# Rotary embedding of two attention layers: partner rows fetched by SBUF-to-SBUF DMAs in place of a TensorE permutation

## The reference, cut to what matters

```python
# layer a: halves of a 64-wide head, also for the index queries qi and the index key ki
def apply_rope(x):
    x1, x2 = x[..., :half], x[..., half:]
    return concatenate([x1 * c - x2 * sn, x1 * sn + x2 * c])

# layer c: neighbours of a head, after an RMS norm of every head
def apply_rope_2(x, cos, sin):
    x1, x2 = xp[..., 0], xp[..., 1]
    return stack([x1 * c - x2 * s, x1 * s + x2 * c])
```

## Time and profile before

| | before |
|---|---|
| median of 3 runs | 2630.72 us (2630.54 to 2632.61) |
| the profiled execution's own time | 2627.3 us |
| its span, first to last instruction | 2626.0 us |
| mean granted TensorE clock | 0.992 |
| PE busy | 2568.1 us (98%) |
| DVE, ACT, POOL busy | 1290.3, 979.4, 1244.5 us |
| DMA | 274.48 MB, mean 105 GB/s |

### The profile page before, as it was taken

How to read it: one execution, slowest core, us unless ns; L and a number is a source line. 1 busy time by engine, 2 the same in 40 slices (tenths; PEclk the granted TensorE clock), 3 DMA queues, 4 the chain that set the end, 5 groups by cost and what they waited for, 6 DMA issues and landing times.

```text
span 2626.0 us, 33091 instructions
## 1 busy us (share of the span) xinstructions
PE 2568.1 (98%) x13418; PEld 2077.3 (79%) x13418; DVE 1290.3 (49%) x2151; ACT 979.4 (37%) x1620; POOL 1244.5 (47%) x618
## 2 busy tenths in 40 slices
PE   8989999999999999999999999999999999999999
PEld 6667888888777888888777888888888888888887
DVE  4873899842135499982566431222336233431221
ACT  4474423223347432233367432232324223432231
POOL 4874544444456444444467344443433443444442
PEclk9999999999999999999999999999999999999999
DMA  4202555532220355542210233322422222233322
GB/s 147 65 18 80 169 192 189 187 106 66 97 80 10 124 189 185 188 157 96 87 35 18 81 96 96 96 97 91 142 96 80 97 88 88 82 96 97 98 98 78
DMA packets 259435, 274.48 MB, mean 105 GB/s; under 512 B 6868, under 2 KB 249300, under 8 KB 259028
## 3 DMA queue, kind: packets, MB, share of 16 engines
q1 hardware_dynamic: 259284, 272.37, 32.1%
HBM read 270.26 MB, written 2.10 MB: 104 GB/s over the span
## 4 chain that ended last, share of the span: by engine, by line
PE 87%; DVE 7%; ACT 2%; issue 2%; POOL 1%; DMA 0%; SPq 0%; DVEq 0%
PE bank L457 22%; PE bank L458 22%; PE bank L459 22%; DVE acc L1394 2%; PE bank L640 2%; PE bank L525 2%; PE bank L527 2%; PE bank L526 2%; PE bank L595 2%; PE bank L433 2%; DVE tmp L1429 2%; PE bank L434 2%; PE bank L437 1%; PE bank L623 1%; DVE Hlo L1432 1%
## 5 line engine op out<-in xcount | busy, mean ns | idle before, releaser
L1738 POOL TENSOR_TENSOR wlo<-raw,whi 128x1024 fp32r<-128x1024 f32 (+1 forms) x408 | 989.4, 2446 | 1192.7 <-ACT whi L926 1192.6
L457 PE MATMUL bank<-Xhi,whi 128*128 128x512 f32 (+1 forms) x1616 | 640.8, 397 | 1.5 <-POOL wlo L1738 1.5
L458 PE MATMUL bank<-Xlo,whi 128*128 128x512 f32 (+1 forms) x1616 | 630.0, 390 | 0.0
L459 PE MATMUL bank<-Xhi,wlo 128*128 128x512 f32 (+1 forms) x1616 | 629.2, 389 | 0.0
L926 ACT ACTIVATE whi<-raw 128x1024 fp32r<-128x1024 f32 (+1 forms) x408 | 404.9, 1041 | 570.0 <-PE bank L459 495.6
L457 PE MATMUL bank<-Hhi,whi 128*128 128x512 f32 x1024 | 400.6, 391 | 0.0
L458 PE MATMUL bank<-Hlo,whi 128*128 128x512 f32 x1024 | 399.0, 390 | 0.0
L459 PE MATMUL bank<-Hhi,wlo 128*128 128x512 f32 x1024 | 398.4, 389 | 0.0
L457 PEld LDWEIGHTS bank<-Xhi,whi 128*128 128x128 f32 (+1 forms) x1616 | 302.2, 187 | 73.5 <-issue 8.1
L459 PEld LDWEIGHTS bank<-Xhi,wlo 128*128 128x128 f32 (+1 forms) x1616 | 302.4, 187 | 65.4
L458 PEld LDWEIGHTS bank<-Xlo,whi 128*128 128x128 f32 (+1 forms) x1616 | 302.4, 187 | 64.9 <-issue 3.2
(11 more groups left out here) (273 smaller groups left out, 3119.0 us busy)
## 6 DMA issues: line engine op xcount, KB each, us to landing
ada<-in_ada_w SPq DMA_DIRECT2D x48, 1024.0 KB, 5.2
raw<-in_w_up SPq DMA_DIRECT2D x32, 1024.0 KB, 5.7
raw<-in_w_down SPq DMA_DIRECT2D x32, 1024.0 KB, 5.1
raw<-in_mlp_w_in SPq DMA_DIRECT2D x32, 1024.0 KB, 5.6
raw<-in_mlp_w_out SPq DMA_DIRECT2D x32, 1024.0 KB, 5.1
raw<-in_gmlp_w_in SPq DMA_DIRECT2D x24, 1024.0 KB, 5.0
raw<-in_gmlp_w_out SPq DMA_DIRECT2D x12, 1024.0 KB, 5.1
raw<-in_w_in_a SPq DMA_DIRECT2D x8, 1024.0 KB, 5.2
```

The costliest lines, as they stand in the source:

```text
L457: pe.matmul(b[0:rows, :], whi[s][:, c, j:j + rows], hi[:, c, :], start=(c == 0), stop=False)
L458: pe.matmul(b[0:rows, :], whi[s][:, c, j:j + rows], lo[:, c, :], start=False, stop=False)
L459: m = pe.matmul(b[0:rows, :], wlo[s][:, c, j:j + rows], hi[:, c, :], start=False, stop=(c == KC - 1))
L1738: pool.tensor_tensor(wlo[u % 2][:, c0:c1, 0:k], src[:, c0:c1, 0:k], whi[u % 2][:, c0:c1, 0:k].bitcast(F32), ALU.subtract).then_inc(lo_done, 1)
```

## The change

Both permutation matrices, their loads and the 25 PE rotations go. A new function `swap(r)` on ACT, called right after the tile has been copied to `held`, waits for that copy, waits until DVE has read the tile of rotation r-3, and issues DMAs from SBUF to SBUF that copy row blocks of the held tile to their partners' partitions: four DMAs of 32 partitions for layer a (two for r = 2), two of every second partition for layer c. They land in one of three new tiles (`SWA`, `SWC`), each with its own semaphore. DVE's sine product reads that tile in place of PSUM bank 4; POOL's cosine product, which works in place, waits for the landing as it waited for PE. For the keys of layer c the swap stands in ACT's order ahead of the evacuation of query tiles 2 and 3.

```diff
+    swap_in = [sem(f"swap_in{i}") for i in range(3)]
...
+    def swap_pieces(r):
+
+        if r >= 15:
+            return [(slice(h, P, 2), slice(1 - h, P, 2)) for h in range(2)]
+        return [(slice(o, o + 32), slice(o ^ 32, (o ^ 32) + 32)) for o in range(0, 64 if r == 2 else P, 32)]
+
+    def swapped(r):
+
+        landed = sum(len(swap_pieces(x)) for x in range(r % 3, r + 1, 3))
+        return (SWA if r < 15 else SWC)[r % 3], swap_in[r % 3], 16 * landed
...
-        def rotation(r, p, rows=P):
-            if r < 15:
-                pe_until.wait_ge(held_in, r + 1)
-            elif ROT_C[r][0] == "q":
-                pe_until.wait_ge(held_in, 18 + ROT_C[r][1])
-            else:
-                pe_until.wait_ge(hn_out, ROT_C[r][1] + 1)
-            if r == 0:
-                pe_until.wait_ge(const_in, 64)
-            else:
-                pe_until.wait_ge(rot_sin, r)
-            pe.matmul(bank[4][0:rows, :], perm[p][0:rows, 0:rows], rotated(r)[0:rows, :], start=True, stop=True).then_inc(rot_full, 1)
-
...
         def after_ki(o):
-            rotation(1, 0)
             pe_until.wait_ge(vec_in, 16 * (len(vec_rows) - 1))
-            pe_until.wait_ge(rot_sin, 2)
...
+        def swap(r):
+
+            tile, landing, _ = swapped(r)
+            if r >= 3:
+                act_until.wait_ge(rot_sin, r - 2)
+            for dst, src in swap_pieces(r):
+                act.dma_start(tile[dst, :], rotated(r)[src, :]).then_inc(landing, 16)
+
         def hold(name, r0, rows=P):
...
                 act.activation(held[r % 3][0:rows, :], bank[g % 4][0:rows, :], ACT_F.Copy).then_inc(held_in, 1)
+                act_until.wait_ge(held_in, r + 1)
+                swap(r)
             return evacuate
...
+            if o in (2, 3):
+                act_until.wait_ge(hn_out, o - 1)
+                swap(ROT_C_AT["k", o - 2])
             wait_tile(g)
...
             act.activation(tmp[o % 2][:], bank[g % 4][:], ACT_F.Square).then_inc(held_in, 1)
+            act_until.wait_ge(held_in, 18 + o)
+            swap(ROT_C_AT["q", o])
         units("qc", evac_qc)
...
         def rotation_sin(r, rope, rows=P):
-            dve_until.wait_ge(rot_full, r + 1)
+            tile, landing, whole = swapped(r)
+            dve_until.wait_ge(landing, whole)
...
-            dve.tensor_tensor(tmp[2 + r % 2][0:rows, :], bank[4][0:rows, :], rope[0:rows, 1, :], ALU.mult).then_inc(rot_sin, 1)
+            dve.tensor_tensor(tmp[2 + r % 2][0:rows, :], tile[0:rows, :], rope[0:rows, 1, :], ALU.mult).then_inc(rot_sin, 1)
...
         def rotation(r, rope, rows=P):
-            pool_until.wait_ge(rot_full, r + 1)
+            _, landing, whole = swapped(r)
+            pool_until.wait_ge(landing, whole)
```

More of the change, by code:

```diff
@@ L143, in body @@
     rcol, zcol, FG, GS = sb("rcol", [P, 2 * NT]), sb("zcol", [P, 2 * NT]), sb("FG", [P, KC]), sb("GS", [P, KC])
-    perm = [sb(f"perm{i}", [P, P]) for i in range(2)]
     pick, warm = sb("pick", [P, 19]), sb("warm", [P, 1])
@@ L195, in body @@
         rope_a = sb("rope_a", [P, 2, S], F32, region)
+        SWA = [sb(f"SWA{i}", [P, S], F32, region) for i in range(3)]
     Hhi, Hlo, ada, gained = [], [], [], None
@@ L215, in body @@
         rope_b = sb("rope_b", [P, 2, S], F32, region)
+        SWC = [sb(f"SWC{i}", [P, S], F32, region) for i in range(3)]
         KH = [sb(f"KH{i}", [P, S], F32, region) for i in range(2)]
@@ L251, in body @@
         sem(n) for n in ("set_done", "xsq_done", "vec_full", "vec_set", "silu_exp", "silu_step"))
-    held_in, rot_full, rot_sin, rot_cos, rot_sum, rot_sump, key_copy, wi_full, wi_set = (
-        sem(n) for n in ("held_in", "rot_full", "rot_sin", "rot_cos", "rot_sum", "rot_sump", "key_copy", "wi_full", "wi_set"))
+    held_in, rot_sin, rot_cos, rot_sum, rot_sump, key_copy, wi_full, wi_set = (
+        sem(n) for n in ("held_in", "rot_sin", "rot_cos", "rot_sum", "rot_sump", "key_copy", "wi_full", "wi_set"))
+    swap_in = [sem(f"swap_in{i}") for i in range(3)]
     idx_full, idx_relu, idx_acc, idx_wt, idx_add, sel_step = (sem(n) for n in ("idx_full", "idx_relu", "idx_acc", "idx_wt", "idx_add", "sel_step"))
@@ L673, in tensor_program @@
         pe_until.wait_ge(vec_set, 1)
-        rotation(0, 0)
         def after_ki(o):
-            rotation(1, 0)
             pe_until.wait_ge(vec_in, 16 * (len(vec_rows) - 1))
-            pe_until.wait_ge(rot_sin, 2)
             pe.transpose(bank[4][:, 0:114], R1, ident[0:114, 0:114]).then_inc(vec_full, 1)
@@ L685, in after_qj @@
             if o:
-                rotation(3, 0)
                 return
@@ L692, in after_qj @@
             m.then_inc(wi_full, 1)
-            rotation(2, 0, 64)
         fm("qj", X, chunk_a, after_qj)
@@ L711, in after_qa @@
         def after_qa(o):
-            rotation(4 + o, 0)
             for i, heads in INDEX_AFTER.get(o, ()):
@@ L715, in tensor_program @@
         fm("qa", X, chunk_a, after_qa)
[L717 to L720, removed]
+        fm("ka", X, chunk_a)
+        tm("va", chunk_a)
         pe_until.wait_ge(idx_relu, 24)
@@ L817, in after_qc @@
             query_means(o - 1)
-            if o in (3, 4):
-                rotation(ROT_C_AT["k", o - 3], 1)
-            rotation(ROT_C_AT["q", o - 1], 1)
         fm("qc", X, lambda c: wait_chunk("c", c), after_qc)
@@ L830, in after_vc @@
                 query_means(7)
-                rotation(ROT_C_AT["q", 7], 1)
             if o == 2:
@@ L1566, in vector_program @@
         dve.tensor_tensor(PBB[7][:].rearrange("p (i c h) -> p i c h", c=8, h=16), *copies, ALU.subtract).then_inc(lf_dve, 1)
-        dve_until.wait_ge(const_in, 64)
+        dve_until.wait_ge(const_in, 32)
         dve.tensor_copy(PICK[:], pick[:, 0:16]).then_inc(ck_dve, 1)
@@ L1862, in sync_program @@
             sp.dma_start(dst, src).then_inc(vec_in, 16)
-        for dst, name in ((head_mean, "head_mean"), (perm[0], "perm_half"), (perm[1], "perm_pair"), (pick, "pick")):
+        for dst, name in ((head_mean, "head_mean"), (pick, "pick")):
             sp.dma_start(dst[:], consts[name]).then_inc(const_in, 16)
@@ L1913, in shape_constants @@
     rope_a = np.stack([np.tile(c, (4, 1)), np.concatenate([-s, s, -s, s])], 1)
[L1914 to L1917, removed]
     tok = np.arange(S)
@@ L1934, in shape_constants @@
         "ident": np.eye(P, dtype=f), "head_mean": np.kron(np.eye(2), np.full((64, 64), 1 / 64)).astype(f),
-        "perm_half": perm_half, "perm_pair": perm_pair, "pick": pick,
+        "pick": pick,
         "rope_a": rope_a.astype(f), "rope_b": rope_b.astype(f), "tri": tri, "tsum": tsum,
```

## The result

| | before | after |
|---|---|---|
| median | 2630.63 us (4 runs, 2629.64 to 2632.61) | 2641.86 us (4 runs, 2639.92 to 2642.22) |
| ratio, 95% interval | | 1.0042 [1.0029, 1.0054] |
| the profiled execution's own time, its span | 2627.3, 2626.0 us | 2641.91, 2640.6 us |
| mean granted TensorE clock | 0.992 | 0.981 |

What follows compares the result with a forecast made beforehand. It took PE to bound layer c and saturated DVE to set layer a's end. Layer a's 4.5 + 1.9 + 5.0 = +11.4 and layer c's -9.8 gave +1.6, so 2632.3 us, range 2620 to 2641 (forecast's own 2626 to 2636).

Steps and rivals of the forecast that it cites:

- The bound: Before the change, PE sets layer c's time; layer a's end is set by 57.3 us of saturated DVE.
- Layer c, -9.8: Layer c: rotations off PE save 10.8 us, 1.0 charged behind the last query tile, ACT's issues otherwise hidden: -9.8 us.
- Layer a, first step, +4.5: Layer a up to the first scores: ACT's issues and DVE's waits for POOL delay rotation 4's sum, +4.5 us.
- Layer a, second step, +1.9: Layer a, query tiles 1 and 2 with scores: ACT's issues delay the relus PE's fourth score waits for, +1.9 us.
- Third step, +5.0: Layer a's saturated DVE stretch: seven sine products wait about 0.8 us each for POOL, +5.0 us.
- The sum: Layer a +11.4 and layer c -9.8 give +1.6 us in the whole kernel, median 2632.3 us.
- (1) PE bounds everything: Whole kernel: all PE savings count, -25 us, some 2606; chance 0.04.
- (2) Layer a breaks even: Layer a: port waits mostly fall in idle moments and ACT's issues are cheap; total -8 to -6, 2623 to 2625; chance 0.23.
- (3) Late landing: POOL's first cosine and layer c's end: swaps land in 5.2 us, not 1.9; total +7.5, 2638; chance 0.23.
- (4) The four pieces land one after the other: A tile's four swap DMAs land serially, 7.6 us; +8.5 on top of +1.6, 2641; chance 0.05.
- The signs: Expected profile marks: no line 577, layer c tiles 6.36 us apart, sine product median near 1.3, memset near 94, attention near 157.

Runs made afterwards that it cites:

- c_only: Only layer c swapped by DMA as in the changed kernel, layer a's rotations left on PE as in the kernel before: 2619.0 us, ratio 0.996.
- filler: Changed kernel plus 60 matmuls with unused results where PE would wait for ACT's relus: 2630.3 us, -11.5 against the changed kernel.
- sp_issue: Changed kernel with layer a's swap DMAs issued by SP between its weight loads instead of ACT: 2626.5 us, -15.3 against the changed kernel.
- port_only: Kernel before, with DVE's sine product of layer a reading two SBUF tiles, no DMA added: 2634.6 us, ratio 1.0019, +4.5.
- psum_sine: Changed kernel with the sine table copied into PSUM bank 4, so the sine product has one PSUM operand: 2637.1 us, -4.8 against the changed kernel.
- sp_psum: Changed kernel with layer a's swaps issued by SP and the sine table copied into PSUM bank 4: 2619.8 us, 22.1 below the changed kernel.
- issue_only: Kernel before plus layer a's 58 DMAs issued by ACT into unread tiles, POOL waiting for their landing: 2640.6 us, ratio 1.004, +10.4.
- one_piece: Changed kernel with one DMA per rotation in layer a, rows copied but not swapped: 2629.05 us, -12.8 against the changed kernel.

## Why the prediction was wrong, point by point

**The bound.** Right in what it read: layer c is PE's, and layer a before the change was DVE's. It took for granted that layer a stays DVE's. After the change the rows from 90 to 140 us show DVE at 1.7 to 6.7 of 10 in three of them: between 77 and 131 us the chain goes through ACT's issues and PE, and only from 134 us on through DVE.

**Layer c, -9.8.** Measured -10.2 in after and in c_only between the same instructions, and -11.1 in c_only's median. Tiles 6.4 apart as worked out (6.36), with or without a key rotation. The issues on ACT cost 1.15 per tile and not 0.9, hidden all the same.

**Layer a, first step, +4.5.** Near in size: the sum of rotation 4 began at 66.07 where 65.6 was worked out, behind DVE's wait of 3.46 for POOL's cosine. Part of that is luck. The `qj` tiles did not end where they were but 4.2 and 3.2 us later (evacuated at 49.40 and 55.43, before 45.19 and 52.21), because PE paused for `wlo`, which the step has at 2.5 us and not 4.0, and then ran 13 matmuls at the low level, which it does not have:

```profile
41.06 0.76 PE L470 MATMUL bank<-Xhi,whi 128*128 128x512 f32 x1 [4.01 <-POOL wlo L1742]
```

So `wlo` began at 59.70 and not 57.9. Against that, cosine 5 did not run ahead of sum 4 but beside it, and held it up: the sum took 1.74 us in place of 0.69 and ended 6.3 us later than before.

**Layer a, second step, +1.9. This is the step that failed**, and with it the third. PE's pause was worked out and charged at its own length, and what comes behind the pause was put at nothing, without a reason. The runs showed TensorE at its low level there for 6 to 7 us: 3.1 us of each tile, by the trace of after and by filler. From rotation 4's sum to the memset it was 33.4 us where it was 26.7, +6.6 in place of +1.9.

The end of the pause came out right by two errors that cancel. The step took 0.37 us per issue, "the row that also moves 64 KB", and 0.43 as the upper bound, both from SP's loads out of DRAM; these SBUF-to-SBUF issues took 0.61 on ACT (0.59 on SP, in sp_issue), so the relu came 3.2 us behind the evacuation and not 2.2. But the step also let the fourth score wait for the second relu. In both kernels (`idx_relu, n - 2`) it waits for the first relu of its four, which comes 1.1 us earlier. So the fourth score could start 3.7 us behind the evacuation, 3.8 by the step; it ended at 5.4 and not at 4.3, because it took 1.65 us at the low level, where 0.5 was put down and 0.91 is what the high level gives.

**Third step, +5.0.** Its mechanism was right: 4.5 us in port_only, 4.8 in psum_sine, the longest product 2.67 us, their mean 1.33. But from the memset to the attention it was 69.3 us in place of 58.6, +10.7. "What PE saves in tiles 3 and later is lost in waiting for DVE" had the wrong sign there: three more tiles came 13.5 to 13.8 us apart (8.8 to 9.5 before), and DVE waited for them. Part of DVE's wait for POOL is hidden by that, so the prices measured one at a time (low clock 11.5 in filler, issues and clock together 15.3 in sp_issue, POOL 4.8 in psum_sine) are not parts of one sum; the last two together gave 22.1 in sp_psum.

**The sum.** +1.6 became +11.2 by medians, and 2641.86 lies just above the range's 2641. Layer a was put at +11.4 and was +22.6 in the trace; the difference, 11.2, is about what filler gives back (11.5) with nothing but a fuller PE. Whether it is that to the last microsecond can't be said: filler also changes when scores come.

**The rivals.** (1) PE bounds everything: false. (2) Layer a breaks even: false. Its "issues on ACT are cheap" is refuted by issue_only. (3) Late landing: false as a cause. Three rotations of 15 did land as late as a weight load, but the median is 2.1 us [1.9 in rows 9], and sp_psum, where landings take up to 4.8 us too, has no loss in layer a. Its sign came out, by another mechanism. (4) The four pieces land one after the other, 7.6 us: false as a delay of landing, since the median piece lands 2.1 us after its own issue and issues are 0.6 apart; that its 2641 is near the measured time is luck. The advice of the Trainium skill's page "DMA: Bandwidth & Descriptors", section "Rules for kernel authors", to use one transfer for two to disjoint partitions, agrees with one_piece in what it saves, 12.8 us, though there by the issues that it spares; one_piece only copies the rows.

**The signs.** No more line 577, ACT's issues between evacuation and relu, tiles of layer c, the maximum of the sine product: as said. Its median in layer a was 0.78 and not 1.3, but the mean of the 128-row products was 1.33: the 0.8 us was worked out as a mean, and some products meet no POOL instruction while others wait for most of one. The memset came at 99 and not 94, the attention at 169 and not 157. The text named an issue cost above 0.5 us as what would make it wrong, and it was above. The low clock was in no sign.

On DVE and POOL the Trainium skill's page "SBUF — State Buffer", section "SBUF: two separate sides", states an exclusive lock: a DVE operation with two SBUF inputs and a GpSimd operation that reads SBUF keep each other out for the whole instruction. By that rule the trace agrees: 0.68 us alone and up to 2.67 beside POOL's `wlo` with two SBUF inputs, never above 0.692 once one of the two lay in PSUM (psum_sine).

## What to carry to other kernels

A DMA issue is work of the engine that issues it, at its own measured price for its kind (0.6 us here, where the loads took 0.30 to 0.43): look at what stands behind it on that engine, and issue from a queue where nobody waits. Where an edit makes PE wait for about two microseconds in every tile, charge the matmuls after the wait at the low level as well (waits of 1.0 to 1.7 us mostly went without it here); filling the wait with matmuls for nothing shows, in one run, how much that is. And where DVE and POOL are both full, keep one operand of DVE's two in PSUM. Before charging a wait, look up in the kernel which increment it waits for.

The two best kernels are c_only, 2619.0 us, which leaves layer a alone, and sp_psum, 2619.8, both 0.4% under before.

## What the runs showed of the hardware that was not expected

TensorE's granted clock fell to its low level, 1.2 of 2.4 GHz, after pauses of PE of only 1.9 to 2.3 us, in four tiles of four (ends at 80.79, 94.24, 107.81 and 121.66), and stayed there for another 6 to 7 us of work, with matmuls 0.43 us apart in place of 0.23, though PE's busy share in the stretch from 80 us was 92%. In one_piece, where PE hardly pauses behind the evacuation, the same stretch had 1.00. In issue_only five pauses of 1.0 to 1.7 us were followed by the low level once, for 3.4 us. The shortest pause in after that was followed by it, and the one in issue_only:

```profile
107.81 1.92 PE L703 MATMUL bank<-KI,QI 64*128 64x512 f32 x2 [1.89 <-ACT TA L1070]
```

```profile
77.48 0.91 PE L720 MATMUL bank<-KI,QI 64*128 64x384 f32 x2 [1.40 <-ACT TA L1088]
```

The issue of an SBUF-to-SBUF DMA of 32 partitions x 2 KB holds the issuing engine for 0.51 us as the first of a group and 0.61 as each next one on ACT, and for a median of 0.59 on SP, where SP's loads of constants took 0.30 to 0.43. In one_piece a single DMA of all 128 partitions, four times the bytes, took 0.47 to 0.51: for these two sizes the bytes hardly matter.
